# Attention values summed on TensorE, probabilities divided on ScalarE, and the first loads and splits of the down product issued earlier, in a hybrid decoder block

## The chip, the cores and the metric

One Trainium2 chip, one of its cores. The metric is the device time of one execution in microseconds (us); lower is better.

## The reference

One layer on x (1024 tokens x 1024, f32) with a conditioning vector c:

```
h   = RMSNorm(x) * (1 + scale1(c)) + shift1(c)
q, k, v, u = h @ W_in                      # 8 query heads, 2 kv heads, head dim 64; u 512 wide
A   = sliding-window attention (window 128), QK norm, partial rotary, a learned sink per head:
      probs = softmax([scores, sink])[..., :-1];  A = probs @ v     # bands of 128 queries x 256 keys
B   = (trailing means over 2/4/8/16 of u, minus u) @ pool_w * pool_scale
x   = x + gate1(c) * (concat[A, B] @ W_o)
x   = x + gate2(c) * (relu(h2 @ W1)^2 @ W2)   # h2: the second modulated norm; hidden width 4096
```

## The kernel before

Each engine has its own program, written out by hand in the order in which its instructions are issued, and semaphores tie the five programs together. There is no scheduler: an instruction that waits holds everything behind it on its engine.

Every f32 product is made of three TensorE passes on operands that are split into a high part (rounded to the type `F32R`) and a low part (value minus high part): hi x hi, hi x lo, lo x hi (`three`, L1974 to L1978). ScalarE makes the high part by a cast (names `hi_...`), VectorE or GpSimd the low part by a subtraction (names `lo_...`), so each operand passes through two engines before TensorE may read it.

The stages, in order of time: (1) the modulation sums and the first tokens' norm; (2) a loop over the eight tiles t of 128 tokens, which for tile t makes the projections u, q and kv on TensorE and between them the attention of tile i = t-2 for both kv heads; (3) the output projection with the attention of tiles 6 and 7; (4) "up", the product with W1 as a seven-product (Strassen-like) scheme over 16 blocks b of 256 hidden units, whose results are kept as seven "quads" per block, stored to a scratch tensor in memory; (5) "down", the product with W2 in the same scheme: 7 phases (`DOWN`: P1, P6, P2, P7, P5, P4, P3) of 16 steps, step n of 112. A step has 12 matmuls of 512 columns.

**Attention of a tile i and a kv head.** TensorE makes the scores (`score`, L2050), VectorE the masked maxima (`maxes`, L1294 to L1305), ScalarE the exponentials with their row sums (`exps`, L778, four heads of 128 x 256 each), VectorE the reciprocal of the sums (`dens`, L1310 and L1314, semaphore `den_ready`), GpSimd one multiplication over all four heads (`normalise`, L1823, semaphore `normed`). TensorE turns the probabilities into PSUM banks 4 and 5 (`turn_p`, L1972 on `probs`), ScalarE and VectorE split them (`hi_pT`, L760; `lo_pT`, L1269), and TensorE multiplies with the values (`attend`, L2029 and L2030). `turn_p` of the second kv head reuses the banks, so it waits for `lo_pT` of the first.

The values are held per kv head as 64 high and 64 low columns side by side. `attend` takes all 128 of them as the stationary operand, so that rows 0 to 63 of the result are v_hi p and rows 64 to 127 v_lo p; a second matmul adds the same with p_lo:

```
both = vv[:, s, kv, :, :].rearrange("p a d -> p (a d)")
mm(attn_bank(i, kv), both, pTh[:, kv, blk, :, :].rearrange("p h q -> p (h q)"), start=blk == 0, stop=False)
```

The two halves of the result have then to be added: ScalarE copies half of each bank to `slots` (`shift_attn`, L769), VectorE adds the other half onto it (`add_attn`, L1280, semaphore `attn_kept`). `project_u(t+1)` on TensorE waits for `attn_kept` of both kv heads of tile t-2, because the bank is used again.

**The order in the loop (tile t, attention tile i = t-2).** TensorE: `project_u(t)`, `score(i, 1)`, `turn_qk(t-1)`, the q projection (24 matmuls), `turn_x(t+1)`, `turn_p(i, 0)`, the kv projection, `turn_p(i, 1)`, `attend(i, 0)`, the pooling windows (L2100), `attend(i, 1)`, `score(i+1, 0)`, `pool_out` (L2073). VectorE between `score(i, 1)` and `lo_pT(i, 0)`: `maxes`, `lo_qk` (L1323), `dens`, up to three pieces of a modulation sum (`add_job_pieces`, L1153), half of `make_h` (L1227), `gain_q` (L1370). ScalarE: `exps(i, 0)`, copies, `hi_qk` (L789, L791), `exps(i, 1)`, `scale_x` (L705), `square_q` (L822), `hi_pT(i, 0)`, `square_kv` (L828), `hi_v`, `hi_pT(i, 1)`, `shift_attn`.

**From up to down.** The last up block (b = 15) and the first down steps overlap. ScalarE casts a step's operands (`hi_step`, L1063), GpSimd makes the low parts of steps 0, 2 and 4 (`POOL_STEPS`, L1939), VectorE of all others (`lo_step`, L1707). In `mix_block` of block 15 VectorE makes `lo_step(1)`, then the sum C12 (L1661), then waits for ScalarE's squares and makes the quads S3, S1, S2, S4 (L1665 to L1672); `lo_step(3)` follows only after them. SyncE issues all loads and stores from one queue. Its buffers for raw operands are a ring of five (`RAWS2`), so `load_step(n)` waits until the low part of step n-5 is made; in block 15 its order is: load 4, store A12, store S3, S1, S2, S4 (each when VectorE or ScalarE has made it), load 5, load 6, ...

Of the kernel before, what the change touches and what calls it, by code (L numbers as in the profile page):

```python
# [16 lines left out]
P = 128  # L17
# [8 lines left out]
HEAD_DIM = 64  # L26
# [27 lines left out]
def build(nc, x, c, positions, w_ada, b_ada, norm1_g, w_in, q_norm_g, k_norm_g, attn_sinks,  # L54
# [30 lines left out]
    with ExitStack() as ctx:  # L85
# [206 lines left out]
        attn_shifted = sem("attn_shifted")  # L292
# [67 lines left out]
        LAST = 4  # L360
        Y_STEPS = ([("U2", j) for j in range(4)] + [(n, j) for j in range(4) for n in ("Y11g", "Y11")]
# [157 lines left out]
        def _(sp):  # L519
# [117 lines left out]
            for b in range(HEAD, NBLK):  # L637
# [17 lines left out]
                if b + 1 == NBLK:  # L655
                    load_step(4)
# [3 lines left out]
            for n in range(RAWS2, STEPS):  # L660
# [28 lines left out]
        def _(act):  # L689
# [72 lines left out]
            def shift_attn(i, kv):  # L762

# [4 lines left out]
                for e in range(2):  # L768
                    ins = nc.scalar.copy(dst[64 * e:64 * e + 64, 2 * kv:2 * kv + 2, :],  # L769
                                         o[64 - 64 * e:128 - 64 * e, :, e, :])  # L770
                ins.then_inc(attn_shifted, 1)

            def exps(i, kv):
# [6 lines left out]
                nc.scalar.activation(es[:, kv * G:kv * G + G], earg[:, kv * G:kv * G + G], ACT.Exp).then_inc(exped, 1)  # L780

# [87 lines left out]
            for t in range(2, NT):  # L869
# [20 lines left out]
                shift_attn(t - 2, 0)  # L890
# [6 lines left out]
                shift_attn(t - 2, 1)  # L897
# [72 lines left out]
            shift_attn(NT - 2, 0)  # L970
# [4 lines left out]
            shift_attn(NT - 2, 1)  # L975
            exps(NT - 1, 0)
            hi_mix(2, 1)
            hi_h2(0, 0)
            exps(NT - 1, 1)
            make_h2_half(0)  # L980
            hi_h2(0, 1)
            square_x2(1)
# [4 lines left out]
            shift_attn(NT - 1, 0)  # L987
# [148 lines left out]
        def _(dve):  # L1136
# [136 lines left out]
            def add_attn(i, kv):  # L1273

                dve.wait_ge(attn_shifted, 2 * i + kv + 1)
                o = attn_bank(i, kv).rearrange("p (m e q) -> p m e q", e=2, q=P)
                for e in range(2):
                    r = slice(64 * e, 64 * e + 64)
                    dst = slots[r, i, :].rearrange("p (m q) -> p m q", q=P)[:, 2 * kv:2 * kv + 2, :]
# [1131 lines left out]
```

## Time and profile before

| | |
|---|---|
| device time, median of 3 runs | 980.75 us (980.31 to 983.38) |
| the profiled execution: its time, its span | 979.74 us, 978.0 us |
| TensorE matmul busy, share of the span | 922.5 us, 94% |
| TensorE weight loads | 763.9 us, 78% |
| VectorE | 677.9 us, 69% |
| ScalarE | 474.7 us, 49% |
| GpSimd | 374.4 us, 38% |
| bytes moved | 175.53 MB, 179 GB/s over the span |
| mean granted clock of TensorE | 0.996 |

A time line gives the start of an instruction or of a merged group, its duration, the engine, the line of the kernel, what it writes and reads, and in brackets the engine's idle time just before it and the instruction that ended it. "PE" is TensorE, "DVE" VectorE, "ACT" ScalarE, "POOL" GpSimd, "SPq" SyncE's queue of transfers. Matmuls overlap in their pipeline, so the distance from start to start, and not the duration, is what one costs.

### The profile page before, as it was taken

Reading aid. Unit: us, or ns where it says so; the run is one execution under the profiler, and the core shown is the slowest. Engines: PE = TensorE matmul, PEld = TensorE weight load, DVE = VectorE, ACT = ScalarE, POOL = GpSimd, SP = SyncE. Lnnn points to the kernel's source line nnn. Section 1 sums busy time; section 2 is a strip of 40 time slices with the busy share of each in tenths; the row PEclk is TensorE's granted clock in tenths of the full one; section 3 lists DMA queues with packets and bytes.
Section 4 is the critical chain, followed back from the end, with each engine's and each line's share of the span. In section 5 each row is a group of like instructions: output and inputs, shape, how many; then the busy total and the mean of one; then the engine's idle time right before and its main releaser. Section 6 shows DMA issues by size and latency. Waiting matters only on the chain.

```text
span 978.0 us, 12577 instructions
## 1 busy us (share of the span) xinstructions
PE 922.5 (94%) x4381; PEld 763.9 (78%) x4381; DVE 677.9 (69%) x1032; ACT 474.7 (49%) x826; POOL 374.4 (38%) x356
## 2 busy tenths in 40 slices
PE   1898899998999999999999999998999999999998
PEld 1687788776778888788887888886877888888787
DVE  6977888888754587655565545444588656789797
ACT  1745556658464564645544554453344444333341
POOL 8052333335332444988888878830000000000000
PEclk9999999999999999999999999999999999999999
DMA  9851432223322240754465435347998637896673
GB/s 357 323 176 53 129 109 65 74 79 129 108 87 86 87 151 29 240 191 165 162 200 187 160 134 163 139 148 253 344 358 313 217 104 243 292 320 225 213 248 120
DMA packets 92270, 175.53 MB, mean 179 GB/s; under 512 B 9320, under 2 KB 26288, under 8 KB 92208
## 3 DMA queue, kind: packets, MB, share of 16 engines
q1 hardware_dynamic: 92096, 174.70, 53.0%
q8 instruction: 35, 0.57, 0.2%
q14 instruction: 27, 0.22, 0.1%
q10 hardware_dynamic: 112, 0.04, 0.0%
HBM read 136.95 MB, written 37.75 MB: 179 GB/s over the span
## 4 chain that ended last, share of the span: by engine, by line
PE 69%; DVE 12%; ACT 6%; DMA 4%; issue 4%; POOL 3%; SPq 1%; DVEq 0%; ACTq 0%; POOLq 0%
PE psum L1976 22%; PE psum L1978 21%; PE psum L1977 21%; DMA down_raw<-in_w_mlp_out 4%; PE psum L1972 2%; DVE down_operands L1707 2%; ACT probs L778 1%; DVE acc L1153 1%; SPq L618 1%; DVE xh L1227 1%; DVE pT_lo L1269 1%; ACT qT L789 1%; PE psum L2073 1%; ACT hT_hi L724 1%; DVE probs L1294 1%
## 5 line engine op out<-in xcount | busy, mean ns | idle before, releaser
L1976 PE MATMUL psum<-down_operands 128*128 128x512 f32 x448 | 176.0, 393 | 5.9 <-DVE down_operands L1707 5.9
L1063 ACT CAST down_operands<-down_raw 128x1024 fp32r<-128x1024 f32 x96 | 100.9, 1053 | 163.1 <-PE psum L1978 60.4
L1978 PE MATMUL psum<-down_operands 128*128 128x512 f32 x448 | 175.1, 391 | 0.0
L1977 PE MATMUL psum<-down_operands 128*128 128x512 f32 x448 | 174.9, 390 | 0.0
L1707 DVE TENSOR_TENSOR down_operands<-down_raw,down_operands 128x1024 fp32r<-128x1024 f32 x93 | 112.9, 1220 | 29.4 <-ACT down_operands L1063 28.4
L1976 PE MATMUL psum<-h2T,w_operands 128*128 128x512 f32 x272 | 107.5, 395 | 1.8 <-DVE act_quads_a L1653 1.3
L1978 PE MATMUL psum<-h2T,w_operands 128*128 128x512 f32 x272 | 106.0, 390 | 0.0
L1977 PE MATMUL psum<-h2T,w_operands 128*128 128x512 f32 x272 | 105.9, 389 | 0.0
L1976 PEld LDWEIGHTS psum<-down_operands 128*128 128x128 f32 x448 | 84.5, 189 | 26.3 <-DVE down_operands L1707 8.8
L1928 POOL TENSOR_TENSOR w_operands<-raw,w_operands 128x512 fp32r<-128x512 f32 x56 | 83.3, 1488 | 42.1 <-ACT w_operands L1015 42.1
L1978 PEld LDWEIGHTS psum<-down_operands 128*128 128x128 f32 x448 | 84.4, 188 | 17.7
L1977 PEld LDWEIGHTS psum<-down_operands 128*128 128x128 f32 x448 | 84.6, 189 | 17.3
L1976 PE MATMUL psum<-w_in_hi,hT_hi 128*128 128x512 f32 (+1 forms) x168 | 61.7, 367 | 4.8 <-issue 2.1
L1978 PE MATMUL psum<-t_sums_hi,w_operands 128*128 128x512 f32 x168 | 65.4, 389 | 0.0
L1976 PE MATMUL psum<-t_sums_hi,w_operands 128*128 128x512 f32 x168 | 65.4, 389 | 0.0
L1977 PE MATMUL psum<-t_sums_lo,w_operands 128*128 128x512 f32 x168 | 65.4, 389 | 0.0
L1976 PEld LDWEIGHTS psum<-h2T,w_operands 128*128 128x128 f32 x272 | 51.0, 188 | 15.7 <-issue 3.8
L1928 POOL TENSOR_TENSOR w_operands<-w_sums,w_operands 128x512 fp32r<-128x512 f32 x42 | 55.9, 1342 | 11.8 <-ACT w_operands L1015 11.8
L1978 PE MATMUL psum<-w_in_hi,hT_lo 128*128 128x512 f32 (+1 forms) x168 | 59.6, 355 | 0.0
L1977 PEld LDWEIGHTS psum<-h2T,w_operands 128*128 128x128 f32 x272 | 51.1, 188 | 10.8 <-issue 0.5
L1978 PEld LDWEIGHTS psum<-h2T,w_operands 128*128 128x128 f32 x272 | 51.1, 188 | 10.8
L1977 PE MATMUL psum<-w_in_lo,hT_hi 128*128 128x512 f32 (+1 forms) x168 | 59.5, 354 | 0.0
(247 smaller groups left out, 1931.9 us busy)
## 6 DMA issues: line engine op xcount, KB each, us to landing
down_raw<-in_w_mlp_out SPq DMA_DIRECT2D x160, 256.0 KB, 4.3
down_raw<-act_scratch SPq DMA_DIRECT2D x112, 256.0 KB, 3.3
raw<-in_w_ada SPq DMA_DIRECT2D x32, 512.0 KB, 4.5
raw<-in_w_mlp_in SPq DMA_DIRECT2D x32, 512.0 KB, 4.8
act_scratch<-act_quads_a SPq DMA_DIRECT2D x64, 256.0 KB, 2.1
act_scratch<-act_quads_b SPq DMA_DIRECT2D x48, 256.0 KB, 3.4
slots<-in_w_ada SPq DMA_DIRECT2D x8, 512.0 KB, 10.6
xh<-in_x SPq DMA_DIRECT2D x8, 512.0 KB, 6.0
```

What stands on the lines that cost most here:

```text
L618: sp.dma_start(raw2[s][:, 1 + j, :], w2[f, i, :, HS * h:HS * h + HS]).then_inc(raw2_in[s], 16)
L724: nc.scalar.copy(hT(t)[0][:, 4 * h:4 * h + 4, :], xh[:, t % 2, 512 * h:512 * h + 512] .rearrange("p (k n) -> p k n", n=P)).then_inc(h_hi, 1)
L778: nc.scalar.activation(pr[:, kv, h, 0:w], pr[:, kv, h, 0:w], ACT.Exp, bias=negm[:, hh:hh + 1], scale=rq(i)[:, hh:hh + 1], accum_out=den[:, ...
L789: nc.scalar.copy(qT[r, :, :].rearrange("p (m e) q -> p m e q", e=2)[:, :, e, :], bank(1)[r, :].rearrange("p (m q) -> p m q", q=P))
L1063: nc.scalar.copy(o[:, 0, :, :], r[:, 0:2, :]).then_inc(op2_hi, 1)
L1153: v.scalar_tensor_tensor(out=target_acc, in0=a, scalar=silu[:, k:k + 1], in1=target_acc, op0=ALU.mult, op1=ALU.add).then_inc(done, 1)
L1707: v.tensor_tensor(o[:, 1, :, :], r[:, 0:2, :], f32(o[:, 0, :, :]), ALU.subtract).then_inc(op2_lo_dve, 1)
L1928: g.tensor_tensor(o[:, 1, :, :], quad, o[:, 0, :, :].bitcast(F32), ALU.subtract).then_inc(w1_lo, 1)
L1972: return nc.tensor.transpose(o, i, ident[0:rows_, 0:rows_])
L1976: mm(o, wh, ah, start=first, stop=False, skip_group_check=adds)
L1977: mm(o, wh, al, start=False, stop=False, skip_group_check=adds)
L1978: return mm(o, wl, ah, start=False, stop=last, skip_group_check=adds)
```

## The change

The parts, as the diff has them:

```diff
@@ ScalarE: scale_x
-                act.wait_ge(x_root, t + 1)
+                act.wait_ge(x_root, max(t, 1))
@@ ScalarE: one copy per 64 partitions, both from rows 0 to 63 of the bank
-            def shift_attn(i, kv):
+            def keep_attn(i, kv):
...
-                                         o[64 - 64 * e:128 - 64 * e, :, e, :])
-                ins.then_inc(attn_shifted, 1)
+                    ins = nc.scalar.copy(dst[64 * e:64 * e + 64, 2 * kv:2 * kv + 2, :], o[0:64, :, e, :])
+                ins.then_inc(attn_kept, 1)
@@ ScalarE: new
+            def normalise(i, kv):
+                act.wait_ge(den_ready, 2 * i + kv + 1)
+                w = P if i == 0 else 2 * P
+                for h in range(G):
+                    ins = nc.scalar.activation(pr[:, kv, h, 0:w], pr[:, kv, h, 0:w], ACT.Copy,
+                                               scale=rden[:, kv * G + h:kv * G + h + 1])
+                ins.then_inc(normed, 1)
@@ VectorE: add_attn(i, kv), two additions of 64 x 256, and its 16 calls are gone
-                    ins = v.tensor_tensor(dst, o[r, :, e, :], dst, ALU.add)
-                ins.then_inc(attn_kept, 1)
@@ GpSimd: normalise and its 16 calls are gone; the first two roots are one
-                g.tensor_tensor(pr[:, kv, :, 0:w], pr[:, kv, :, 0:w], bcast(rden[:, r], 2, w), ALU.mult).then_inc(normed, 1)
-            root_x(0)
-            root_x(1)
+            pool.wait_ge(x_squared, 2)
+            root(rx[:, 0:2], ssx[:, 0:2], D, x_root)
@@ TensorE: attend
+                o = attn_bank(i, kv)[0:HEAD_DIM, :]
                 for blk in range(blocks):
+                    pe.wait_ge(pT_hi, p_blocks(i, kv, blk))
...
-                    both = vv[:, s, kv, :, :].rearrange("p a d -> p (a d)")
-                    mm(attn_bank(i, kv), both, pTh[:, kv, blk, :, :].rearrange("p h q -> p (h q)"), start=blk == 0, stop=False)
-                    ins = mm(attn_bank(i, kv), both, pTl[:, kv, blk, :, :].rearrange("p h q -> p (h q)"), start=False,
-                             stop=blk == blocks - 1)
+                    mm(o, vv[:, s, kv, 0, :], hi, start=blk == 0, stop=False)
+                    mm(o, vv[:, s, kv, 1, :], hi, start=False, stop=False)
+                    pe.wait_ge(pT_lo, p_blocks(i, kv, blk))
+                    ins = mm(o, vv[:, s, kv, 0, :], lo, start=False, stop=blk == blocks - 1)
@@ SyncE, last up block (AHEAD = 9)
                 if b + 1 == NBLK:
-                    load_step(4)
+                    for n in range(4, AHEAD):
+                        load_step(n)
                 store_quad(b, "A12")
...
-            for n in range(RAWS2, STEPS):
+            for n in range(AHEAD, STEPS):
@@ VectorE, mix_block, after the sum C12
+                if b + 1 == NBLK:
+                    lo_step(3)
                 dve.wait_ge(c11_kept, kept_count(b))
...
-                if n > 1 and n not in POOL_STEPS:
+                if n > 3 and n not in POOL_STEPS:
                     lo_step(n)
```

The matmul that used v_lo with p_lo is gone, and a block of keys has three matmuls of 64 output rows where it had two of 128. In the loop ScalarE's `normalise(i, 0)` stands between `scale_x` and `square_q`, `normalise(i, 1)` between `square_q` and `hi_pT(i, 0)`. ScalarE's program for one tile of the loop (t = 6), before:

```order
L778 ACTIVATE probs,small<-probs,small 128x256 x4
L780 ACTIVATE small<-small 128x4
L705 ACTIVATE xh<-xh,small 128x1024
L822 ACTIVATE squares<-psum 128x512
L760 CAST pT_hi<-psum 128x512 x2
L828 ACTIVATE squares<-psum 128x128
```

and with the change:

```order
L777 ACTIVATE probs,small<-probs,small 128x256 x4
L779 ACTIVATE small<-small 128x4
L706 ACTIVATE xh<-xh,small 128x1024
L785 ACTIVATE probs<-probs,small 128x256 x4
L829 ACTIVATE squares<-psum 128x512
L785 ACTIVATE probs<-probs,small 128x256 x4
L761 CAST pT_hi<-psum 128x512 x2
L835 ACTIVATE squares<-psum 128x128
```

The casts that TensorE and VectorE need for `lo_pT` now stand behind both divisions. SyncE's queue in the last up block (the number behind `down_raw` is the buffer, steps 4 to 9 use buffers 4, 0, 1, 2, 3, 4), before:

```order
L615 DMA down_raw4<-act_scratch 128x512
L618 DMA down_raw4<-in_w_mlp_out 128x512
L603 DMA act_scratch<-act_quads_a 128x512
L603 DMA act_scratch<-act_quads_b 128x512
L603 DMA act_scratch<-act_quads_a 128x512
L603 DMA act_scratch<-act_quads_b 128x512 x2
L615 DMA down_raw0<-act_scratch 128x512
L618 DMA down_raw0<-in_w_mlp_out 128x512
```

and with the change:

```order
L615 DMA down_raw4<-act_scratch 128x512
L618 DMA down_raw4<-in_w_mlp_out 128x512
L615 DMA down_raw0<-act_scratch 128x512
L618 DMA down_raw0<-in_w_mlp_out 128x512
L615 DMA down_raw1<-act_scratch 128x512
L618 DMA down_raw1<-in_w_mlp_out 128x512
L615 DMA down_raw2<-act_scratch 128x512
L618 DMA down_raw2<-in_w_mlp_out 128x512
L615 DMA down_raw3<-act_scratch 128x512
L618 DMA down_raw3<-in_w_mlp_out 128x512
L603 DMA act_scratch<-act_quads_a 128x512
L603 DMA act_scratch<-act_quads_b 128x512
```

Four loads of two transfers each now stand ahead of the five stores. VectorE's program at the same place (`down_operands3` is written by `lo_step(3)`), before:

```order
L1707 TENSOR_TENSOR down_operands1<-down_raw1,down_operands1 128x1024
L1661 TENSOR_TENSOR act_quads_a<-psum,up_temps 128x512
L1665 TENSOR_TENSOR act_quads_b<-act_quads_a 128x512
L1666 TENSOR_TENSOR act_quads_a<-act_quads_a 128x512
L1669 TENSOR_TENSOR act_quads_b<-act_quads_a 128x512
L1672 TENSOR_TENSOR act_quads_b<-act_quads_a,act_quads_b 128x512
L1707 TENSOR_TENSOR down_operands3<-down_raw3,down_operands3 128x1024
L1707 TENSOR_TENSOR down_operands5<-down_raw0,down_operands5 128x1024
```

and with the change:

```order
L1705 TENSOR_TENSOR down_operands1<-down_raw1,down_operands1 128x1024
L1657 TENSOR_TENSOR act_quads_a<-psum,up_temps 128x512
L1705 TENSOR_TENSOR down_operands3<-down_raw3,down_operands3 128x1024
L1663 TENSOR_TENSOR act_quads_b<-act_quads_a 128x512
L1664 TENSOR_TENSOR act_quads_a<-act_quads_a 128x512
L1667 TENSOR_TENSOR act_quads_b<-act_quads_a 128x512
L1670 TENSOR_TENSOR act_quads_b<-act_quads_a,act_quads_b 128x512
L1705 TENSOR_TENSOR down_operands5<-down_raw0,down_operands5 128x1024
```

`lo_step(3)` has moved from behind the four quads to ahead of them.

## Rows read from the trace of the kernel before

**Rows 1.** Stretches: length, busy time of each engine, granted clock, DMA share, GB/s.

```profile
118.00:122.00 4.00, 2.45 (x14) 2.21 (x15) 4.00 (x10) 1.07 (x2) 0.42 (x2) 0.86 0.45 134
122.00:126.00 4.00, 4.00 (x22) 3.78 (x22) 3.29 (x8) 3.19 (x7) 1.74 (x1) 0.71 0.00 0
234.00:246.00 12.00, 9.85 (x49) 7.27 (x49) 10.88 (x28) 11.41 (x28) 7.44 (x4) 1.00 0.51 171
665.00:670.00 5.00, 3.77 (x17) 2.79 (x15) 1.34 (x3) 3.35 (x5) 2.41 (x1) 1.00 0.14 52
680.00:740.00 60.00, 59.28 (x258) 47.95 (x258) 43.33 (x50) 24.69 (x27) 0.00 (x0) 1.00 1.00 354
```

**Rows 2.** Who TensorE waited for: total us, number of waits, longest.

```profile
PE psum L1972 <- DVE pT_lo L1269: 8.7, 5, 2.5
```

**Rows 3.** Time line of TensorE: two matmuls of `attend` back to back; waits.

```profile
119.55 1.06 PE L1972 MATMUL psum<-ident,probs 128*128 128x128 f32 x8 [2.47 <-DVE pT_lo L1269]
...
199.81 1.06 PE L1972 MATMUL psum<-ident,probs 128*128 128x128 f32 x8 [1.65 <-DVE pT_lo L1269]
...
206.39 0.47 PE L1976 MATMUL psum<-w_in_hi,hT_hi 128*128 128x512 f32 x1 [0.51 <-issue]
...
250.14 0.39 PE L2030 MATMUL psum<-pT_lo,vv 128*128 128x512 f32 x1
250.37 0.39 PE L2029 MATMUL psum<-pT_hi,vv 128*128 128x512 f32 x1
...
279.54 0.66 PE L1972 MATMUL psum<-ident,hx 128*128 128x128 f32 x4 [0.53 <-ACT hx L910]
...
280.82 0.47 PE L2029 MATMUL psum<-pT_hi,vv 128*128 128x512 f32 x1 [0.63 <-DVE pT_lo L1269]
```

**Rows 4.** Time line of VectorE in the loop, tile t = 6.

```profile
183.13 2.60 DVE L1153 SCALAR_TENSOR_TENSOR acc<-raw,small,acc 128x1024 f32<-128x1024 f32 x2
...
192.48 4.10 DVE L1153 SCALAR_TENSOR_TENSOR acc<-raw,small,acc 128x1024 f32<-128x1024 f32 x2
...
198.39 1.27 DVE L1269 TENSOR_TENSOR pT_lo<-psum,pT_hi 128x512 fp32r<-128x512 f32 x2
...
205.44 0.85 DVE L1280 TENSOR_TENSOR slots<-psum,slots 64x256 f32<-64x256 f32 x2
```

**Rows 5.** Time line of GpSimd, same tile: the division of the second kv head.

```profile
192.65 2.86 POOL L1823 TENSOR_TENSOR probs<-probs,small 128x1024 f32<-128x1024 f32 x1 [3.44 <-DVE small L1314]
```

**Rows 6.** ScalarE's groups, shapes apart: busy us, mean ns, idle before them.

```profile
L778 ACT ACTIVATE probs<-probs,small 128x256 f32<-128x256 f32 x56 | 33.0, 592 | 28.9 <-DVE small L1305 28.9
...
L791 ACT CAST kT<-psum 128x256 fp32r<-128x256 f32 x8 | 3.0, 374 | 0.1
```

**Rows 7.** Time line of ScalarE in tile t = 6.

```profile
192.06 1.14 ACT L705 ACTIVATE xh<-xh,small 128x1024 f32<-128x1024 f32 x1
...
195.32 1.08 ACT L760 CAST pT_hi<-psum 128x512 fp32r<-128x512 f32 x2 [1.47 <-PE psum L1972]
```

**Rows 8.** Time line of TensorE from up to down, and the first wait after.

```profile
672.62 0.50 PE L1976 MATMUL psum<-down_operands 128*128 128x512 f32 x1 [3.86 <-DVE down_operands L1707]
...
677.30 0.40 PE L1977 MATMUL psum<-down_operands 128*128 128x512 f32 x1
...
735.83 0.50 PE L1976 MATMUL psum<-down_operands 128*128 128x512 f32 x1 [0.72 <-DVE down_operands L1707]
```

**Rows 9.** Time lines of ScalarE, VectorE and SyncE's queue around the same place.

```profile
657.76 1.05 ACT L1063 CAST down_operands<-down_raw 128x1024 fp32r<-128x1024 f32 x1 [3.07 <-DMA down_raw<-in_w_mlp_out]
...
660.64 0.69 DVE L1661 TENSOR_TENSOR act_quads_a<-psum,up_temps 128x512 f32<-128x512 f32 x1 [0.90 <-PE psum L1978]
...
671.36 1.22 DVE L1707 TENSOR_TENSOR down_operands<-down_raw,down_operands 128x1024 fp32r<-128x1024 f32 x1
...
660.87 1.74 SPq L618 DMA_DIRECT2D down_raw<-in_w_mlp_out  x1
...
671.88 0.40 SPq L615 DMA_DIRECT2D down_raw<-act_scratch  x1
```

More of the change, by code:

```diff
@@ L360, in build @@
         LAST = 4
+        AHEAD = 9
         Y_STEPS = ([("U2", j) for j in range(4)] + [(n, j) for j in range(4) for n in ("Y11g", "Y11")]
@@ L880, in _ @@
                     scale_x(t + 1)
+                normalise(t - 2, 0)
                 square_q(t)
@@ L883, in _ @@
                     hi_qk(1)
+                normalise(t - 2, 1)
                 hi_pT(t - 2, 0)
@@ L889, in _ @@
                 hi_pT(t - 2, 1)
-                shift_attn(t - 2, 0)
+                keep_attn(t - 2, 0)
                 if t + 1 < NT:
@@ L896, in _ @@
                 keep_pooled(t)
-                shift_attn(t - 2, 1)
+                keep_attn(t - 2, 1)
             hi_wo(1)
@@ L962, in _ @@
             hi_qk(NT - 1)
+            normalise(NT - 2, 0)
             hi_wo(5)
@@ L965, in _ @@
             hi_wo(6)
+            normalise(NT - 2, 1)
             hi_pT(NT - 2, 0)
@@ L969, in _ @@
             hi_mix(1, 1)
-            shift_attn(NT - 2, 0)
+            keep_attn(NT - 2, 0)
             hi_pT(NT - 2, 1)
@@ L974, in _ @@
             hi_mix(2, 0)
-            shift_attn(NT - 2, 1)
+            keep_attn(NT - 2, 1)
             exps(NT - 1, 0)
@@ L978, in _ @@
             hi_h2(0, 0)
+            normalise(NT - 1, 0)
             exps(NT - 1, 1)
@@ L981, in _ @@
             hi_h2(0, 1)
+            normalise(NT - 1, 1)
             square_x2(1)
@@ L986, in _ @@
             hi_mix(3, 1)
-            shift_attn(NT - 1, 0)
+            keep_attn(NT - 1, 0)
             hi_h2(1, 0)
@@ L1068, in _ @@
                 if i == 3:
-                    shift_attn(NT - 1, 1)
+                    keep_attn(NT - 1, 1)
                 if i == 7:
@@ L1271, in lo_pT @@
                                     ALU.subtract).then_inc(pT_lo, 1)
[L1273 to L1279, printed above, removed]
-                    ins = v.tensor_tensor(dst, o[r, :, e, :], dst, ALU.add)
-                ins.then_inc(attn_kept, 1)
             def maxes(i, kv):
@@ L1442, in _ @@
                 lo_pT(t - 2, 1)
-                add_attn(t - 2, 0)
                 if t + 1 < NT:
@@ L1448, in _ @@
                     lo_h(t + 1, 1)
-                add_attn(t - 2, 1)
                 if t == NT - 1:
@@ L1507, in _ @@
             make_x2(0)
-            add_attn(NT - 2, 0)
             lo_mix(1, 1)
@@ L1512, in _ @@
             maxes(NT - 1, 0)
-            add_attn(NT - 2, 1)
             dens(NT - 1, 0)
@@ L1523, in _ @@
             make_x2(2)
-            add_attn(NT - 1, 0)
             lo_pT(NT - 1, 1)
@@ L1606, in _ @@
                     lo_mix(i + 1, 0)
-                if i == 3:
-                    add_attn(NT - 1, 1)
                 make_h2_half(i - 1)
@@ L1842, in _ @@
             for t in range(NT):
-                if t >= 2:
-                    normalise(t - 2, 0)
                 if t == 1:
@@ L2023, in attend @@
                 blocks = 1 if i == 0 else 2
+                o = attn_bank(i, kv)[0:HEAD_DIM, :]
                 for blk in range(blocks):
[L2025 to L2031 removed]
+                    pe.wait_ge(pT_hi, p_blocks(i, kv, blk))
+                    s = (i if blk == i % 2 else i - 1) % 4
+                    hi, lo = (a[:, kv, blk, :, :].rearrange("p h q -> p (h q)") for a in (pTh, pTl))
+                    mm(o, vv[:, s, kv, 0, :], hi, start=blk == 0, stop=False)
+                    mm(o, vv[:, s, kv, 1, :], hi, start=False, stop=False)
+                    pe.wait_ge(pT_lo, p_blocks(i, kv, blk))
+                    ins = mm(o, vv[:, s, kv, 0, :], lo, start=False, stop=blk == blocks - 1)
                 ins.then_inc(pv_done, 1)
```

13 lines of the change are left out of this document (removed).

## The prediction

> **What bounds the kernel now.** I read the page first: TensorE is 94% busy, so only two things change the time: matmuls added or taken, and the some 55 us in which TensorE stands idle or runs at a lower clock. The waits by engine say where the idle time in the loop is: 8.7 us in 5 waits end with VectorE's `pT_lo` [rows 2]. TensorE's time line then gives each wait its place [rows 3]: `turn_p(i, 1)` waited 2.47 us at t = 3 and 1.65 us at t = 6 (between them stand 1.91 and 1.16, before them 1.49 at t = 2). A smaller wait, 0.51 us, stands ahead of `project_u(t+1)`; its line names no releaser, but in the code it waits for `attn_kept`, and VectorE's second `add_attn` ended at 205.44 + 0.85 = 206.29, just before 206.39 [rows 3, 4]. Four tiles have this wait. The largest single wait is at the seam from up to down, 3.86 us [rows 8]. There are also stretches at a lower clock: mean 0.86 and 0.71 in the 8 us behind the 2.47 us wait [rows 1], and thirteen matmul starts in 677.30 - 672.62 = 4.68 us behind the 3.86 us wait, where 13 x 0.227 = 2.95 us is usual [rows 8]. Both are TensorE at 1.2 GHz for some us after an idle time.
>
> **The sum**, against the profiled execution (979.74 us for a span of 978.0).
>
> *a. Matmuls of `attend`.* 60 become 90. One costs the distance between two starts, 250.37 - 250.14 = 0.23 us (0.227 over longer runs) [rows 3]. 30 x 0.227 = **+6.8 us**, all on TensorE, which is the bound. No row has 64 output rows; half price would be +3.4 and a clumsy switch at each group some 0.1 us more. I take the full price, since the 512 moving columns are the same. That the first two may now start ahead of `pT_lo` gains nothing in the loop: TensorE comes there late, after `turn_p(i, 1)`.
>
> *b. The wait for `pT_lo` in the loop, t = 3 to 6.* VectorE's two modulation pieces take 2.60 us at 183.13 and 4.10 us at 192.48 [rows 4]. In the second case GpSimd's division runs from 192.65 to 195.51 [rows 5], and VectorE's second piece stands still until it ends. All four tiles have one such piece of 2.8 us instead of 1.28. Without a division on GpSimd VectorE is 1.5 us earlier in each. But `lo_pT` also needs ScalarE's casts, and these now stand behind two divisions. Per head I bound the new operation by a 128 x 256 cast, 374 ns, and the exponential with its row sum, 592 ns [rows 6]; having no sum to read it is nearer the cast: 0.42, so 1.7 us per kv head. At t = 6: `scale_x` ends at 193.2 [rows 7], division 194.9, `square_q` 195.5, division 197.2, casts 198.25, where they ended at 196.4 [rows 7]. VectorE would be ready at 198.39 - 1.5 = 196.9 [rows 4], so it waits for the casts and finishes `lo_pT` at 198.9 instead of 199.66: 0.8 us. The same count gives 1.4, 1.0 and 0.8 us for t = 3, 4, 5. Together **-4.0 us**; ends 0 and -6.0.
>
> The Trainium skill (SBUF — State Buffer, "SBUF: two separate sides") says VectorE and GpSimd share one port pair, held for a whole instruction, and that ScalarE has its own. The trace agrees for the one pair (2.80 us against 1.28 for the same piece). By that rule the hold goes away wholly and does not come back on ScalarE. The same notes (VectorE: DVE Perf Modes, "The TRN2 errata") speak against the change: for SBUF data ScalarE pays 224 cycles at 1.2 GHz per instruction and one per column, so four instructions of 256 columns cost 1.6 us where one of 1024 would cost 1.04. That estimate is 0.40 per head, and the sum by it would be 0.16 us better per tile, 0.6 us in all.
>
> *c. The wait for `attn_kept`.* VectorE's additions are gone and ScalarE's copy ends about 1 us earlier; with 0.9 us more of TensorE work ahead of it, four waits of 0.51 vanish: **-2.0 us** (ends 0 and -2.0).
>
> *d. Tiles t = 2 and t = 7.* They have no held pieces, so ScalarE's extra 1.7 us per head group shows: +0.2 and +0.7; at t = 7 a later wait of TensorE for VectorE's pooled sums takes it up again. **0**, ends -0.5 and +1.5.
>
> *e. Behind the loop, 234 to 246.* ScalarE is busy 11.41 of 12 us there [rows 1] and gets two divisions, 3.4 us; `hi_wo(5)`, `hi_wo(6)`, `hi_wo(7)` stand behind them and `project_out(0, k)` waits for those parts. VectorE's missing `add_attn` brings the start of this chain forward by 0.85 us, and GpSimd no longer has two divisions between its own parts. I take **+1.2 us**, ends 0 and +2.5. Behind 246 ScalarE has idle time, so the delay ends there.
>
> *f. 279 to 283.* TensorE waited 0.53 and 0.63 us [rows 3] behind GpSimd's last division, which delayed a root, a scaling and `hi_pT`. Gone: **-1.2 us** (0 to -1.4).
>
> *g. The clock at t = 3.* The dip costs (0.14 + 0.29) x 4 = 1.7 us [rows 1]. The wait ahead of it falls from 2.5 to about 1 us; the waits of 1.91 and 1.65 us were followed by no dip. I take it as gone: **-1.5 us**; ends 0 and -1.7.
>
> *h. The seam.* The high part of step 3 is ready at 657.76 + 1.05 = 658.8 and the sum C12 at 661.3, but the low part was made only at 671.36 [rows 9]. Now it is made at 661.3 to 662.6, TensorE reaches step 3 at 668.8 and does not wait: -3.86, and the dip behind the wait, 4.68 - 2.95 = 1.7, goes too. What is late next: step 5, needed two steps of 12 x 0.227 = 2.7 us later, at 674.2. Its load was issued at 671.88 [rows 9]; now four loads go out between 662.6 and 666.5, when the DMA engines are 0.14 busy [rows 1]. ScalarE casts it by 669.5, VectorE reaches it behind the quads at 671.4 and is done at 672.6: in time. Store A12, now behind these loads, went out at 667.3, so it isn't delayed, and nobody needs it soon. From 680 to 740 the DMA engines are full (1.00) [rows 1] and TensorE waits for them once, 0.72 us at 735.83 [rows 8]. They start 4 loads of 512 KB ahead, 2.1 MB at 354 GB/s = 5.9 us, about as much as TensorE gains; 0.2 us may be lost: **-5.4 us**, ends 0 and -6.
>
> *i. The first two roots as one* on GpSimd: a column more per instruction, one pair less, +-0.2: **0**.
>
> Sum: 6.8 - 4.0 - 2.0 + 0 + 1.2 - 1.2 - 1.5 - 5.4 = **-6.1 us**, 973.6 for an execution like the profiled one. The median of the runs is 1.0 us above that execution, so I forecast **974.0 us** for the median.
>
> **The rivals.**
>
> 1. *ScalarE becomes the bound (slower).* If a division costs what an exponential does, 0.592, four take 2.4 us, and `hi_pT` is 1.4 us later than above in each tile. The point from which it decides is 0.54 per head: there b is nothing. At 0.592 b becomes +1.6, g stays out, d is +2.5, e +2.6, f -0.7: 6.8 + 1.6 - 2.0 + 2.5 + 2.6 - 0.7 - 5.4 = +5.4, **986**. For it: 8 of the 16 groups lie directly on that chain. Against: 592 ns holds a row sum.
>
> 2. *The seam's gain goes to the DMA.* The engines are full for 60 us, and the wait at 735.83 shows that TensorE is no slower than they are. If the early loads don't bring the later ones forward, the 5.4 us appear again as waits in P6: **979.5**. Against: the 0.14 in 665 to 670.
>
> 3. *The loop gives nothing back.* VectorE's lead is eaten by the casts, and the dip stays: without b and g -0.6, **979.3**.
>
> 4. *More than summed*: VectorE's other small operations are freed of GpSimd too, e is hidden and b is full: **969.5**.
>
> 5. *The change doesn't do what it says*, in that a matmul with 64 output rows has half the price: 3.4 us less, **970.5**.
>
> **How the numbers follow.** Forecast 0.60, rival 1 0.07, rival 2 0.09, rival 3 0.12, rivals 4 and 5 0.12. 0.3% of 980.75 is 2.9 us, about what a measurement of this kernel can tell from no change. Faster than 977.8: 0.60 less 0.02 at its rim, and 0.12, so 0.70 with what rivals 2 and 3 leave when only part of them comes true, 0.72. Within: 0.20. Slower than 983.7: 0.08. The range from 969.0 to 980.0 takes in rivals 2 to 5 and the ends of most terms, and leaves out rival 1.
>
> **What would show it.** In the changed profile: 90 matmuls of `attend` at 0.227 us from start to start; no VectorE piece of 2.8 us in the loop; the division on ScalarE near 0.42 us from start to start (above 0.54 rival 1); waits for `pT_lo` of some 4 us in sum instead of 8.7; no 0.51 us ahead of `project_u`; a wait of TensorE between 238 and 250 of about 1 us more; granted clock 1.00 at 118 to 126; no wait at the seam, and one below 1 us in P6 (5 us there: rival 2). I am wrong if the stretch from 45 to 300 grows by more than it did by a, or if a new wait stands in down.

## The result and the profile after

The changed kernel took **972.43 us** (median of 5 runs, 971.58 to 977.41), the kernel before on the same chip 982.52: a ratio of 0.9914 with a 95% interval of [0.9895, 0.9933]. By the ratio that is 8.5 us less (the medians lie 10.1 us apart), well beyond the 0.3% that can be told from no change. Measured once more beside the experiments: 973.84 against 982.45, 0.9909 [0.9887, 0.9932]. The execution that was profiled is the slowest of its five, 977.41 us for a span of 975.7. It is 3.0 us slower than the profiled execution of the repeat (e5, 974.38 us): 1.7 us of that lie ahead of the first `project_u` and 1.6 us at steps 90 to 93 of down, where the most useful thing in this case stands.

| | before | after |
|---|---|---|
| TensorE busy, instructions | 922.5 us (94%), x4381 | 929.0 us (95%), x4411 |
| VectorE busy | 677.9 us | 655.2 us |
| ScalarE busy | 474.7 us | 497.5 us |
| GpSimd busy | 374.4 us | 340.9 us |

The groups that the prediction spoke of, in the changed kernel's profile. First the stretches, in the columns of [rows 1], with two more of down at the end:

```profile
118.00:122.00 4.00, 3.70 (x27) 3.00 (x26) 4.00 (x9) 1.74 (x6) 0.67 (x2) 1.00 0.46 176
122.00:126.00 4.00, 4.00 (x29) 3.47 (x29) 2.81 (x9) 2.85 (x7) 1.61 (x2) 1.00 0.01 2
234.00:246.00 12.00, 8.58 (x35) 5.30 (x34) 7.27 (x16) 10.93 (x26) 4.74 (x2) 1.00 0.54 167
665.00:670.00 5.00, 5.00 (x23) 4.13 (x22) 4.09 (x6) 4.45 (x5) 0.66 (x1) 1.00 1.05 396
680.00:740.00 60.00, 58.95 (x256) 47.30 (x255) 45.02 (x52) 25.11 (x27) 0.00 (x0) 1.00 0.97 343
910.00:915.00 5.00, 2.81 (x7) 2.23 (x8) 4.93 (x7) 2.09 (x2) 0.00 (x0) 0.64 0.79 287
915.00:920.00 5.00, 5.00 (x17) 3.95 (x16) 4.96 (x7) 2.62 (x3) 0.00 (x0) 0.67 0.70 211
```

The clock at 118 to 126 is whole now, where [rows 1] had 0.86 and 0.71. Between 234 and 246 TensorE does less in the same 12 us: 8.58 against 9.85. At the seam (665 to 670) TensorE is busy throughout and the DMA engines are full. The last two rows are new: TensorE at 0.64 and 0.67 of its clock, far behind the last place that the prediction looked at.

Who TensorE waited for (total, times, longest), to be held against [rows 2]:

```profile
PE psum L1960 <- DVE down_operands L1705: 5.2, 3, 4.1
...
PE psum L1956 <- ACT probs L785: 3.8, 6, 1.9
...
PE psum L1956 <- DVE pT_lo L1282: 1.8, 2, 1.5
...
PE psum L1960 <- POOL w_o_lo L1831: 0.9, 1, 0.9
```

The 8.7 us behind `pT_lo` have become 1.8, of which 1.49 is at t = 2, where it was before too. In its place stands a wait for ScalarE's division (L785). The time line of TensorE, columns as in [rows 3]:

```profile
119.30 1.06 PE L1956 MATMUL psum<-ident,probs 128*128 128x128 f32 x8 [0.30 <-DVE pT_lo L1282]
...
191.31 1.09 PE L1956 MATMUL psum<-ident,probs 128*128 128x128 f32 x8 [0.44 <-ACT probs L785]
195.27 1.06 PE L1956 MATMUL psum<-ident,probs 128*128 128x128 f32 x8
...
200.89 1.05 PE L2059 MATMUL psum<-pooledT,pool_w 128*128 128x128 f32 x8
201.69 0.48 PE L1960 MATMUL psum<-w_in_hi,hT_hi 128*128 128x512 f32 x1
...
236.66 1.09 PE L1956 MATMUL psum<-ident,probs 128*128 128x128 f32 x8 [1.86 <-ACT probs L785]
...
240.05 0.50 PE L1960 MATMUL psum<-w_o_hi,mixT_hi 128*128 128x512 f32 x1 [0.90 <-POOL w_o_lo L1831]
...
245.74 0.50 PE L1960 MATMUL psum<-w_o_hi,mixT_hi 128*128 128x512 f32 x1 [0.66 <-DVE w_o_lo L1332]
...
912.19 0.80 PE L1960 MATMUL psum<-down_operands 128*128 128x512 f32 x1 [4.13 <-DVE down_operands L1705]
912.79 0.63 PE L1961 MATMUL psum<-down_operands 128*128 128x512 f32 x1
```

In tiles t = 3 to 6 `turn_p(i, 0)` waits 0.44 us for the division, `turn_p(i, 1)` 0.30 us at t = 3 and nothing after. The wait ahead of `project_u` (201.69) is gone. Behind the loop stand three waits, 3.4 us in sum. One names ScalarE; the other two name GpSimd and VectorE, whose low parts need a cast of ScalarE's first, and ScalarE is busy 10.93 of 12 us there (e7 tests this reading). And at 912.19 stands the longest wait that down has in either profile, with matmuls behind it that last 0.63 us instead of 0.39.

The division itself, ScalarE's time line at t = 6:

```profile
191.63 1.71 ACT L785 ACTIVATE probs<-probs,small 128x256 f32<-128x256 f32 x4
193.23 1.06 ACT L761 CAST pT_hi<-psum 128x512 fp32r<-128x512 f32 x2
```

Each of the four rows lasts 0.50 us by itself, but the four together last 1.71: they start (1.71 - 0.50) / 3 = 0.40 us apart. What four in a row cost is the distance of the starts, and 0.42 had been assumed.

And the cause of the wait at 912, first in SyncE's queue, then on VectorE:

```profile
890.23 0.33 SPq L615 DMA_DIRECT2D down_raw<-act_scratch  x1
890.59 0.91 SPq L618 DMA_DIRECT2D down_raw<-in_w_mlp_out  x2
891.54 11.59 SPq L627 DMA_DIRECT2D out<-x_quads  x4
903.24 0.85 SPq L615 DMA_DIRECT2D down_raw<-act_scratch  x1
```

```profile
902.08 0.69 DVE L1733 TENSOR_TENSOR x_quads<-y_temps,x_quads 128x512 f32<-128x512 f32 x1
909.58 0.69 DVE L1693 TENSOR_TENSOR down_raw<-down_raw,w_sums 128x512 f32<-128x512 f32 x1 [6.81 <-DMA down_raw<-in_w_mlp_out]
910.31 0.69 DVE L1695 TENSOR_TENSOR down_raw<-down_raw 128x512 f32<-128x512 f32 x1
910.92 1.22 DVE L1705 TENSOR_TENSOR down_operands<-down_raw,down_operands 128x1024 fp32r<-128x1024 f32 x1
```

`store_out(1, 4, 1, "Y22")` stands in SyncE's program behind the load of step 92. Each of its four stores waits for one of VectorE's gathers, so they take 11.6 us to go out (L627), and the load of step 93 behind them leaves only at 903.24. VectorE makes the sum for step 93 *before* the low half of step 91. So VectorE idles 6.81 us for that load, the low half of step 91 ends at 912.14, and TensorE waits at step 91. The kernel before has the same order and the same wait, 1.36 us in its profiled execution.

**Where the time went**, from the starts of the same TensorE instruction in each profile (us; only differences from one landmark to the next; "steps" are of down, 12 matmuls each, and three steps without a wait take 8.16):

| stretch | before | after | after, again (e5) | sum on TensorE only (e3) | division only (e4) | both, no down part (e2) | down part only (e1) |
|---|---|---|---|---|---|---|---|
| up to the first `project_u` | 35.85 | 37.93 | 36.23 | 36.05 | 37.86 | 36.24 | 36.08 |
| to the last `pool_out(7)` | 193.52 | 187.62 | 187.66 | 193.37 | 188.80 | 187.66 | 194.26 |
| to step 0 | 431.07 | 432.44 | 432.50 | 431.49 | 432.70 | 432.41 | 431.25 |
| step 0 to 30 | 89.45 | 83.99 | 84.10 | 88.95 | 89.24 | 88.23 | 83.99 |
| step 30 to 90 | 163.20 | 163.20 | 163.20 | 163.20 | 163.19 | 163.20 | 163.20 |
| step 90 to 93 | 9.83 | 15.43 | 13.85 | 13.59 | 10.26 | 12.98 | 12.32 |

One profile of each is not enough for differences of a microsecond. Six profiles have the loop of the kernel before (before, e1, e9 to e12); it lasts 192.9, 192.9, 193.5, 194.2, 194.3 and 195.4 us in them. With both attention parts (after, e2, e5, e6, e7) it lasts 187.6 to 187.7 in all five. Steps 0 to 30 without the down part take 88.2 to 89.5 us in five profiles (before, e2, e3, e4, e9), and before's 89.45 is the longest of them; with the whole down part they take 83.0 to 85.5 in seven.

### The profile page after: what moved, and what is told of

Its sections match the earlier page's. It is cut to its first block, busy times and chain, and to the rows that moved or that the text cites. A ratio compares the mean times of both kernels' runs of the same rounds, so it can differ in the third digit from the quotient of the medians.

```text
span 975.7 us, 12651 instructions
## 1 busy us (share of the span) xinstructions
PE 929.0 (95%) x4411; PEld 766.3 (79%) x4411; DVE 655.2 (67%) x1000; ACT 497.5 (51%) x890; POOL 340.9 (35%) x338
## 4 chain that ended last, share of the span: by engine, by line
PE 67%; DVE 11%; ACT 7%; DMA 6%; issue 3%; POOL 2%; SPq 2%; DVEq 0%; ACTq 0%; POOLq 0%
PE psum L1960 20%; PE psum L1962 20%; PE psum L1961 20%; DMA down_raw<-in_w_mlp_out 6%; PE psum L1956 3%; DVE down_operands L1705 2%; ACT probs L777 2%; ACT probs L785 1%; SPq L618 1%; PE psum L2036 1%; DVE down_raw L1693 1%; ACT qT L796 1%; POOL band L1791 1%; PE psum L2086 1%; PE psum L2017 1%
## 5 line engine op out<-in xcount | busy, mean ns | idle before, releaser
L1818 POOL TENSOR_SCALAR small<-small 128x1 f32<-128x1 f32 (+2 forms) x23 | 8.2, 357 | 176.5 <-DVE small L1366 111.8
```

## The experiments

**e1, the down part alone.** On the kernel before:

```diff
+        AHEAD = 9
-                    load_step(4)
+                    for n in range(4, AHEAD):
+                        load_step(n)
-            for n in range(RAWS2, STEPS):
+            for n in range(AHEAD, STEPS):
+                if b + 1 == NBLK:
+                    lo_step(3)
                 dve.wait_ge(c11_kept, kept_count(b))
-                if n > 1 and n not in POOL_STEPS:
+                if n > 3 and n not in POOL_STEPS:
```

> The kernel before with the down product's part alone (steps 5 to 8 loaded ahead, low half of step 3 made ahead of the last differences). My sum: the seam is worth 5.4 us by itself, so 0.5 to 0.6% below the kernel before, no wait at step 3, and no wait above 1 us at steps 16 to 92. Rival (the gain goes to the DMA): within 1 us of the kernel before, with some 5 us of new waits in the steps of P6. A third possibility, from the profile of the changed kernel, where one boundary (P5 to P4, about 912 us) had a wait of 4.13 us and a stretch at half clock: an execution with that wait gives back up to 5.6 us, one without it keeps all of the gain.

Measured: 977.79 us against 981.06, 0.9957 [0.9940, 0.9974]. Steps 0 to 30 took 83.99 us, 5.46 less than before, with no wait at the seam and 0.3 us more in P6. Rival 2 is out. Of these 5.5 us only 3.3 reach the median; the profile shows 2.5 us more lost at 90 to 93 than before's had, with a wait of 2.25 us where none above 1 us was expected, and before's own profile is a long one at the seam (see above).

**e2, the attention part alone** (the changed kernel without the lines above).

> The changed kernel with the down product as before (attention, division and the merged roots alone). My sum: +6.8 - 4.0 - 2.0 + 1.2 - 1.2 - 1.5 = -0.7 us. The changed kernel's profile was 2.45 us ahead at the first step of down, so -2.5 us if nothing else moves. Rival (the loop gives nothing back): +5 us. If the gain of the whole were all the seam's, this one would be within 1 us of the kernel before.

Measured: 978.95 against 981.06, 0.9973 [0.9960, 0.9986]. The median is 2.1 us lower, near the second of the two expectations. In the trace the part from the first `project_u` to step 0 is 4.5 us shorter, more than either; at steps 90 to 93 it loses 3.15 us more than before. The merged roots are in it, and its first `project_u` is at 36.24: the 37.93 of the changed kernel's profile is not their work. There sixteen transposes took 3.67 us instead of 2.20; e4's profile, which has the roots apart, and e8's have the same, and e5's, the same kernel as the changed one, has 2.20 again.

**e3, the sum on TensorE alone**: `attend` with three matmuls and `keep_attn`, the division left on GpSimd. **e4, the division on ScalarE alone**: `shift_attn` and `add_attn` left as they were.

> The sum of the attention output on TensorE alone, the division left on GpSimd, roots and down product as before. My terms a and c: 6.8 - 2.0 = +4.8 us. If the later TensorE also hides part of the waits for the low parts (they depend on VectorE's chain, not on TensorE), less: +1 to +3 us. Rival: +6.8 if the waits for the kept attention output come back elsewhere; +1.4 if a matmul with 64 output rows costs half.

> The division on ScalarE alone; attention output summed by VectorE and down product as before. My terms b, e, f, g: -4.0 + 1.2 - 1.2 - 1.5 = -5.5 us. With the measured 0.50 us per head instead of 0.42, the casts end some 0.6 us later per tile and b is about -2: -3.5 us. Rival (ScalarE becomes the bound): 0 or slower, waits of TensorE for ScalarE's probabilities in the loop in place of those for the low parts.

Measured: e3 981.70, 1.0008 [0.9996, 1.0020]; e4 978.31, 0.9968 [0.9956, 0.9979]. So thirty more matmuls on the busiest engine, with the waits that this edit removes, cost 0.6 us, which is not clear of noise, where +4.8, or +1 to +3, was expected. The division alone (e4) gives 2.75 us, where 5.5 or 3.5 was expected. In the table e3's loop is as long as before's (-0.15), and 3.0 had been the sum for it (22 of the 30 matmuls, less 2.0). Both have one stretch at half clock in the loop; against the profiles of e1 and e12, which have one too, e3's loop is 0.8 to 0.9 shorter. The waits for `pT_lo` are all still there:

```profile
PE psum L1952 <- DVE pT_lo L1266: 8.8, 5, 2.5
```

What is gone is the wait ahead of `project_u`, and it was worth more than its row said. From the last group of `pool_out` to the first matmul of `project_u` it is 206.39 - 204.72 = 1.67 us before (the first row below is of the kernel before, the second is the one in [rows 3]) and 201.69 - 200.89 = 0.80 after: **0.87 us for a wait listed as 0.51**, since the listed idle time begins only where the modelled end of the matmuls before it lies, and 0.1 of the 0.87 lies inside the group of `pool_out`.

```profile
204.72 1.16 PE L2073 MATMUL psum<-pooledT,pool_w 128*128 128x128 f32 x8
```

The division alone gives 4.7 us in the loop and costs 1.6 behind it. Together (e2, after) the loop is 5.9 shorter, 1.0 more than the two parts add up to, which is less than profiles of one and the same loop differ by.

**e5, the changed kernel again; e6, its stores of Y22 four steps later; e7, also the divisions of tile i = 6 back on GpSimd; e8, each division cut in two.** e6 is one line:

```diff
-                if n == 92:
+                if n == 96:
                     store_out(1, 4, 1, "Y22")
```

e7 has in addition GpSimd's `normalise` as it was, called for `NT - 2` alone, ahead of `lo_wo(5)` and behind `lo_wo(6)`, and not on ScalarE there. e8:

```diff
                 for h in range(G):
-                    ins = nc.scalar.activation(pr[:, kv, h, 0:w], pr[:, kv, h, 0:w], ACT.Copy,
-                                               scale=rden[:, kv * G + h:kv * G + h + 1])
+                    for a in range(0, w, P):
+                        ins = nc.scalar.activation(pr[:, kv, h, a:a + P], pr[:, kv, h, a:a + P], ACT.Copy,
+                                                   scale=rden[:, kv * G + h:kv * G + h + 1])
```

> The changed kernel itself once more, as the measure for the three that follow. The parts alone gave -3.3 us (down part) and -2.1 us (attention part) by their medians: if they add up, 975.7 us against 981.1 for the kernel before. By the first runs (972.43 against 982.52) it would be 10 us below the kernel before. The wait at the boundary of P5 and P4 should again lie between 1.3 and 4.2 us; where it is above 2.3, a stretch at half clock follows it.

> The changed kernel with the four stores of Y22 in SyncE's queue behind the load of step 96 instead of step 92. Theory: the wait ahead of step 93 (1.36 us before, 4.13 in the changed kernel's profile, 1.8 to 3.5 in the four experiments so far) is the load of step 93 queued behind stores that wait for VectorE's gathers. Then the wait is below 0.5 us, no half clock follows, and the time is 1.4 to 7 us below the changed kernel's, 4 us by the middle of the five profiles. Rival: VectorE's own work (four gathers and two sums per step) is late there; then the wait stays above 1.3 us and the time is the same.

> As the one before, and the two divisions of the tile before the last (i = 6) back on GpSimd. Theory (my term e): behind the loop ScalarE is the bound, and turn_p(6,0), project_out(0,5) and project_out(0,7) wait for it, 1.86 + 0.90 + 0.66 us; turn_p(6,1) stood 23.07 us behind the last pool_out where it stood 21.46 before and 20.92 with the division on GpSimd. Expected: about 21.5, so 1.5 us less than the one before. Rival: GpSimd's 2.9 us division holds VectorE there and delays its own two low parts; then no gain.

> The changed kernel with each division of 256 columns made as two of 128 columns, to make the price of a division on ScalarE about 0.59 us per head (the 128-column one lasts 391 ns, the 256-column one 498, and four of the latter start 0.40 apart). That is the price in my first rival, which gave 12 us above my forecast (986 against 974). If the sum's slope is right, +8 to +12 us over the changed kernel, with waits for ScalarE in every tile of the loop; if the loop has room for it, less than +4 us.

| | us | ratio to before (982.45) | 95% | steps 90 to 93 |
|---|---|---|---|---|
| e5 | 973.84 | 0.9909 | [0.9887, 0.9932] | 13.85 |
| e6 | 968.76 | 0.9866 | [0.9842, 0.9889] | 8.16 |
| e7 | **965.80** | 0.9840 | [0.9816, 0.9863] | 8.16 |
| e8 | 983.90 | 1.0016 | [0.9996, 1.0037] | 11.16 |

e5: by the medians the parts do not quite add up; it is 8.6 us below before where e1 and e2 gave 5.4. The three intervals are 1.3 to 2.2 us to either side, so this can be noise. In the traces they do add up: the loop gives 5.9 in e2 as here, the seam 5.5 in e1 and 5.4 here.

e6: the theory holds (the texts on record say "step 93", and some "the boundary of P5 and P4"; the late load is that of step 93, the step that waits is 91, by VectorE's order, and both lie inside P4). Its queue sends the loads one by one and the stores in 2.4 us behind the load of step 96:

```profile
894.50 0.33 SPq L615 DMA_DIRECT2D down_raw<-act_scratch  x1
894.87 0.91 SPq L618 DMA_DIRECT2D down_raw<-in_w_mlp_out  x2
896.96 0.33 SPq L615 DMA_DIRECT2D down_raw<-act_scratch  x1
897.33 0.91 SPq L618 DMA_DIRECT2D down_raw<-in_w_mlp_out  x2
902.02 0.33 SPq L615 DMA_DIRECT2D down_raw<-act_scratch  x1
902.39 0.43 SPq L618 DMA_DIRECT2D down_raw<-in_w_mlp_out  x1
902.86 2.37 SPq L627 DMA_DIRECT2D out<-x_quads  x4
```

The load of step 93 leaves at 894.50 instead of 903.24; 2.1 of the 8.7 us are this execution's earlier step 90, so the stores had held it up by some 6.7 us. In the time line of TensorE from 886 to 914 no wait is left, and the clock is 1.00 in 905 to 920.

e7: behind the loop ScalarE was the bound. `turn_p(6, 1)` stands 244.41 - 223.49 = 20.92 us behind the last `pool_out`, where it stood 23.07 in the changed kernel and 21.46 before. The waits there, in the same view as above:

```profile
233.15 1.07 PE L1961 MATMUL psum<-ident,probs 128*128 128x128 f32 x8 [0.42 <-DVE small L1306]
...
234.80 0.50 PE L1965 MATMUL psum<-w_o_hi,mixT_hi 128*128 128x512 f32 x1 [0.58 <-DVE w_o_lo L1330]
...
237.04 0.50 PE L1965 MATMUL psum<-w_o_hi,mixT_hi 128*128 128x512 f32 x1 [0.59 <-POOL w_o_lo L1834]
```

1.59 us instead of 3.42. By the medians it is 3.0 us better than e6, where 1.5 was expected; the intervals of e6 and e7 overlap. By the two profiles it is 3.0 as well: 2.1 behind the loop, where the edit is, 0.5 ahead of the first `project_u` and 0.4 in P6, which the edit does not touch.

e8: 10.1 us slower than e5, and no faster than the kernel before. ScalarE's group is now

```profile
194.40 2.44 ACT L786 ACTIVATE probs<-probs,small 128x128 f32<-128x128 f32 x8
```

eight starts (2.44 - 0.39) / 7 = 0.29 us apart, 0.59 per head: the price of rival 1, which gave 12 us. The waits in the loop, from 45 to 229:

```profile
PE psum L1957 <- ACT probs L786: 5.7, 5, 1.2
PE psum L1957 <- DVE pT_lo L1283: 5.2, 6, 1.5
```

In the trace the loop is 194.79 us long (+7.1), the part behind it up to step 0 is 2.7 longer. So the loop has no slack on ScalarE: 0.19 us more per head costs 10 us.

**e9 to e12, the down part taken apart, with the spread of steps 90 to 93 removed.** All four have e6's line on the kernel before. e9 has nothing else. e10 adds the whole down part. e11 adds only `lo_step(3)` ahead of the differences, with `AHEAD = 5`. e12 adds only the loads, with `AHEAD = 8`, and leaves `lo_step(3)` where it was.

> The kernel before with nothing but the four stores of Y22 behind the load of step 96. The wait at step 93 is there in the kernel before too: its profile lost 1.7 us there (9.83 us for three steps that take 8.16). Then 1.7 us less than before if its other runs lose as much, and up to 4 us less if they lose what the profiles of the experiments lost. It is the measure for the next three, in which the spread from that boundary should be gone. If the change made the wait worse, the gain here is clearly below the 5.1 us that the same edit gave on the changed kernel.

> The one before with the whole down part (loads of steps 5 to 8 ahead, low half of step 3 early). My term h says 5.4 us less than the one before, of it 3.86 the wait and 1.7 the slow clock behind it; the traces of the changed kernel and of the down part alone say 5.8 at the seam less 0.3 to 0.5 in P6. Rival 2 (the DMA takes it back in P6) would show less than 2 us here. What is left to the attention part is this one less the changed kernel with late stores (13.7 us below before): by my sum 0.7 us, by the traces 4.3.

> Of the down part only the low half of step 3 ahead of the last differences; loads 5 to 8 where they were. The wait of step 3 goes, but the load of step 5 is issued behind five stores at 671.9; it lands near 673.8, cast by 674.9, low half by 676.2, and TensorE wants step 5 at 674.2. So a new wait of about 2 us at step 5: 3 to 4 us below the late-stores kernel (half clock behind the new wait would make it 2), 2 us short of the whole down part. Rival: loads are no matter, then it equals the whole down part.

> Of the down part only the loads of steps 5 to 7 ahead (step 8 needs the low half of step 3, so not that one); the low half of step 3 stays behind the differences. Theory: step 3 is late because of VectorE's order and not of a load, so the wait of 3.9 us stays and the time is that of the late-stores kernel, within 1 us. Rival (the DMA sets the time of P6, and an earlier start of the loads is the gain): 3 us or more below.

| | us | ratio to before (981.63) | 95% | step 0 to 30 | 90 to 93 | wait in TensorE's time line |
|---|---|---|---|---|---|---|
| e9 | 978.79 | 0.9973 | [0.9959, 0.9986] | 88.59 | 8.16 | 3.47 at step 3 |
| e10 | 975.08 | 0.9930 | [0.9914, 0.9946] | 85.47 | 8.16 | none over 1.0 |
| e11 | 978.82 | 0.9975 | [0.9962, 0.9988] | 89.14 | 8.16 | 3.57 at step 5 |
| e12 | 977.65 | 0.9952 | [0.9934, 0.9970] | 88.56 | 8.16 | 4.27 at step 3 |

e9: the order of the stores costs the kernel before 2.8 us by the medians. e10: the down part gives 3.7 us more by the median, 3.1 by this trace, against 5.5 in e1 and in the changed kernel. Of the 2.3 between them 1.0 is taken back in P6 (steps 18 to 30 last 36.05 us against 35.0 in both of those), 0.45 in steps 0 to 18, and 0.9 is the shorter stretch of e9, 88.59 against before's 89.45. e11: the wait does not go, it moves. With the low half of step 3 made early alone, TensorE stands at step 5 instead, for longer than the 2 us expected. Its load leaves at 673.92, which is no later than before's if the later step 0 of this execution (662.75, 2.3 us later) is taken off; but the cast begins 3.8 us behind it, and 1.9 had been reckoned:

```profile
680.08 0.80 PE L1978 MATMUL psum<-down_operands 128*128 128x512 f32 x1 [3.57 <-DVE down_operands L1709]
...
673.92 0.40 SPq L615 DMA_DIRECT2D down_raw<-act_scratch  x1
...
677.72 1.04 ACT L1063 CAST down_operands<-down_raw 128x1024 fp32r<-128x1024 f32 x1 [7.26 <-DMA down_raw<-in_w_mlp_out]
```

e12: with the loads alone step 3 waits as before. Steps 0 to 18 even take 55.92 us, but P6 runs without a wait (32.64 for steps 18 to 30, twelve steps of 2.72), so nothing is lost either. **The two edits are worth 3.7 us together, nothing (e11) and 1.1 us (e12) by themselves.** The intervals of e9 and e10 do not touch; those of e9 and e12 overlap, so the 1.1 is not clear of noise.

## Why the prediction was right, point by point

The number was right (974.0 forecast; 972.4 and 973.8 measured, inside 969 to 980) and so was the sign, but two parts of the sum were off by some 3 to 5 us in opposite directions: the loop gained more than forecast, and steps 90 to 93, which the sum had at 0, lost. That they nearly cancelled is luck. The sum itself, -6.1 on a median of 980.75, is 974.65; the forecast says 974.0, and no row accounts for the 0.6. By the same count rivals 2 and 3 lie at 980.05 and 980.15, just outside the stated range that was to hold them.

- **a, right.** 90 matmuls of `attend`, 0.23 us from start to start with 64 output rows as with 128. Rival 5 is out.

```profile
120.44 0.39 PE L2015 MATMUL psum<-pT_hi,vv 128*64 128x512 f32 x1
120.67 0.39 PE L2017 MATMUL psum<-pT_lo,vv 128*64 128x512 f32 x1
```

- **b, right in kind, a little small.** The waits of t = 3 to 6 were 7.2 us and are 0.30, and 0.44 each, 0.20 at t = 7, has come at `turn_p(i, 0)`, which the sum did not name: 4.9 us net against 4.0. No VectorE piece of 2.8 us is left. The division costs 0.40 where 0.42 was assumed. The Trainium skill (VectorE: DVE Perf Modes, "The TRN2 errata") gives 0.40 by its 224 cycles and one per column at 1.2 GHz. The trace agrees, if starts are taken and not the 0.50 us of each row; it also agrees for 128 columns, 0.29.
- **c, the step that failed.** "four waits of 0.51 vanish: -2.0 us". They vanished, but each was worth 0.87 us from start to start (0.76 at t = 2), and at t = 3, where none was listed, the distance fell by 0.17 as well: 3.5 in sum. e3, which has this edit without the division, shows it: -0.15 us in the loop instead of +3.0. Of the 3.1 us between them 1.5 are this, and 1.1 are smaller waits that a later TensorE meets less: for the pooled sums 1.1 us in sum instead of 1.9, at `turn_p(2, 1)` 1.65 instead of 1.91. The rest lies ahead of `pool_out`, which waits for `attn_kept` too: in tiles t = 4 to 6 it starts 0.12 us behind the last matmul of `score` where it started 0.35 behind, 0.7 in sum with almost no idle time listed (0.07 each). These add up to 3.3, which is as near to 3.1 as two profiles allow. So the term was mis-sized at -2.0: with everything that goes away with the additions it is about -5.
- **d, right.** t = 2 and t = 7 show no loss.
- **e, right.** The stretch from `pool_out(7)` to `turn_p(6, 1)` is 1.6 longer; 0.45 of it are two matmuls of `attend` that term a has counted, so +1.2 as forecast. It is undone by e7.
- **f, right.** From `turn_p(6, 1)` to `turn_p(7, 1)` 31.07 became 30.35, with 0.9 us more of `attend` in it, so -1.6 against -1.2.
- **g, right in result, but it was priced from one execution.** The clock is 1.00 at 118 to 126. The stretch at half clock there is no fixed part of the kernel before, though: of the six profiles with its loop, all with the same wait at t = 3, four have it (before, e1, e11, e12) and two do not (e9, e10). The rows of e9, with full clock behind the wait:

```profile
120.08 1.07 PE L1972 MATMUL psum<-ident,probs 128*128 128x128 f32 x8 [2.47 <-DVE pT_lo L1269]
...
118.00:122.00 4.00, 1.92 (x13) 1.78 (x14) 4.00 (x10) 0.90 (x3) 0.00 (x0) 1.00 0.47 154
122.00:126.00 4.00, 3.92 (x29) 3.50 (x27) 3.86 (x9) 3.35 (x8) 2.17 (x2) 1.00 0.00 0
```

  e3 is as e9 here (1.00 from 118 to 145, a wait of 2.48) and has 0.94 in 198 to 225 instead. The prediction's remark that the waits of 1.91 and 1.65 us are followed by no dip does not hold either: in e11 the clock is 0.57 in 147 to 151, behind the 1.92 us. In the profiles without the division on GpSimd (after, e2, e4 to e8) the loop has none. That fits the shorter waits, but which execution gets one, and so what the shorter wait was worth, is left open.
- **h, right in kind, its size only by the one profile.** 5.46 us in the trace against 5.4, with 5.8 at the seam and 0.34 lost in P6 as assumed. But before's profile is the slowest of the five without the down part; between the means of those five and of the seven with it lie 4.9 us, and in the medians 3.3 to 3.7.
- **i, right.** The roots show nothing (e2).
- **Missed altogether: steps 90 to 93.** The sum had 0 there, although a new wait in down was named as a sign of being wrong; this one is old but grew. The profiled execution lost 5.6 us more than before's, the repeat 4.0. It was in the profile of before: a wait of 1.36 us at 917, and stores that took 11.6 us to go out, from 898.06 to 909.65. The prediction read only the waits next to the edits and the first one behind them.

Whether the change makes this stretch worse is not settled. The late stores gave 5.1 us on the changed kernel and 2.8 on the kernel before, but the intervals overlap, and in the eight profiles with the stores at step 92 the loss is anything from 1.7 to 7.3 us, in all six with them at step 96 it is 0.00. What sets it from run to run was not tried.

Rival 1 was a real danger: e8 shows it at its price. Rival 3 is out (5.9 us in the loop). Rival 4 comes nearest to what happened in the loop, rival 2 to what e10 shows of P6.

## What to carry to other kernels

Price a wait by the distance between the starts around it, not by its listed idle time; a work-adding edit on the busiest engine can be free if it removes such waits. Before costing an edit that makes an engine earlier, read every wait that it will reach afterwards, and in each queue look for a long issue of something that waits for a computation (here four stores, 11.6 us) with loads behind it: moving one line past four loads gave 5.1 us here and 2.8 us on the kernel before, where the whole down part gave 3.3 to 3.7. Compare several profiles before a difference of a microsecond is read from two. And a gain at a seam may need two edits at once, since the second-latest operand stands right behind the latest.

## What the runs showed of the hardware

Single rows on ScalarE overlap: 128 x 256 with a scale lasts 0.50 us and starts every 0.40, 128 x 128 0.39 and 0.29. The clock fell to half (matmul starts 0.43 us apart in 912.79 to 917.91) behind a wait of 4.13 us in the changed kernel, and it stayed at 1.00 behind the 1.36 us of the kernel before at the same place. In between, the length of the wait did not tell. At steps 90 to 93 half clock followed 2.25 us in e1, and e8 kept full clock behind a longer one:

```profile
921.09 0.50 PE L1961 MATMUL psum<-down_operands 128*128 128x512 f32 x1 [2.71 <-DVE down_operands L1706]
...
921.00:926.00 5.00, 4.91 (x22) 4.07 (x23) 4.93 (x8) 2.13 (x3) 0.00 (x0) 1.00 0.66 207
```

The text on record for e5 expected half clock behind every wait above 2.3 us there; that does not hold. At the seam a wait of 2.59 us (e2) had half clock behind it (0.66 in 667 to 672) and one of 2.60 us (e3) had none (1.00 in 672 to 677). At steps 90 to 93 half clock cost 1.9 us on top of the wait in e1, e2, e3 and e5 and 3.1 us in the changed kernel's profile; without it 0.3 us were lost on top (before, e4, e8).
